# One core, a streaming encoder layer with 64 experts: two accumulators in HBM for even and odd blocks, empty places passed over, one gate product moved ahead

## What is computed

```python
def moe(x, w_router, router_bias, w_exp_gu, w_exp_down, w_sh_gu, w_sh_down):
    scores = jax.nn.sigmoid(jnp.einsum("td,de->te", xt, w_router))
    _, idx = lax.top_k(scores + router_bias, MOE_TOPK)          # 6 of 64 experts
    gate = jnp.take_along_axis(scores, idx, axis=-1)
    gate = gate / gate.sum(-1, keepdims=True) * ROUTED_SCALE
    routed = routed_experts(xt, idx, gate, w_exp_gu, w_exp_down)
    shared = swiglu(xt, w_sh_gu, w_sh_down)
    return (routed + shared).reshape(B, L, D)
# x <- LN2(ALPHA*x + MoE(x))
```

## Time and profile before

| | us |
|---|---|
| time before, median of 3 | 2080.77 (2078.91 to 2081.96) |
| the profiled execution: its own time | 2079.63 |
| its span | 2077.8 |
| PE busy | 1959.6 (94%) |
| DVE, ACT, POOL busy | 929.9, 562.7, 618.8 |
| expert loop, first product to last | 1269.5 to 2030.1 |
| from there to the span's end | 47.7 |

### The profile page before, as it was taken

One profiled execution on the slowest core, in us unless ns is written; L12 is line 12 of the kernel. 1 busy time (PEld: TensorE's weight loads), 2 busy tenths in 40 slices (PEclk: granted clock), 3 DMA queues, 4 the chain that ended last, 5 costly groups with the idle time before them and its releaser, 6 DMA issues.

```text
span 2077.8 us, 23451 instructions
## 1 busy us (share of the span) xinstructions
PE 1959.6 (94%) x7658; PEld 1084.7 (52%) x7658; DVE 929.9 (45%) x2467; ACT 562.7 (27%) x1147; POOL 618.8 (30%) x792
## 2 busy tenths in 40 slices
PE   8998999999999999999999899999999999999990
PEld 6786645666555665556555463444444444444440
DVE  4374465999765533030344743233332332332324
ACT  2223554562566640030233000111111111111114
POOL 0042000101220001101223254545445555555444
PEclk9999999999999999999999999999999999999995
DMA  6031212110110011134211406999999999999995
GB/s 189 3 38 14 64 41 102 41 47 5 26 26 3 1 31 48 44 132 126 103 61 48 155 31 217 376 369 373 381 373 375 378 373 376 375 373 377 375 364 193
DMA packets 130467, 365.09 MB, mean 176 GB/s; under 512 B 34641, under 2 KB 82514, under 8 KB 112594
## 3 DMA queue, kind: packets, MB, share of 16 engines
q1 hardware_dynamic: 105250, 289.80, 37.2%
q0 software_dynamic: 23328, 72.90, 13.6%
q10 hardware_dynamic: 1808, 1.33, 0.2%
HBM read 310.82 MB, written 53.04 MB: 175 GB/s over the span
## 4 chain that ended last, share of the span: by engine, by line
PE 55%; DMA 19%; DVE 8%; issue 7%; POOL 7%; ACT 2%; POOLq 0%; SPq 0%; DVEq 0%; ACTq 0%
DMA arena<-x_d,tid 17%; PE psum L630 11%; PE psum L774 9%; PE psum L792 6%; PE psum L645 4%; POOL arena L1293 3%; PE psum L845 3%; PE psum L444 3%; POOL acc_d L1287 2%; PE psum L479 2%; PE psum L708 2%; ACT arena L1341 2%; DVE arena L2264 2%; DMA acc_d<-arena,sid 2%; PE psum L491 2%
## 5 line engine op out<-in xcount | busy, mean ns | idle before, releaser
L1341 ACT ACTIVATE arena<-psum 128x512 f32<-128x512 f32 (+8 forms) x643 | 286.0, 486 | 1086.6 <-PE psum L918 429.7
L918 PE MATMUL psum<-arena 128*128 128x512 f32 x1088 | 484.3, 598 | 27.8 <-DVE arena L2264 24.9
L918 PEld LDWEIGHTS psum<-arena 128*128 128x128 f32 x1088 | 201.6, 190 | 267.2 <-issue 265.0
L1293 POOL DMA_INDIRECT arena<-x_d,tid x276 | 264.9, 960 | 85.8 <-issue 71.3
L932 PE MATMUL psum<-arena 128*128 128x512 f32 x544 | 244.7, 593 | 0.5 <-ACT arena L1341 0.5
L630 PE MATMUL psum<-arena 128*128 128x384 f32 (+1 forms) x768 | 239.7, 471 | 0.2 <-DMA arena<-in_w_glu 0.2
L2314 DVE TENSOR_TENSOR arena<-arena,psum 128x256 f32<-128x256 f32 x68 | 28.6, 421 | 457.7 <-ACT arena L1341 457.7
L630 PEld LDWEIGHTS psum<-arena 128*128 128x128 f32 x768 | 144.5, 190 | 94.7 <-issue 10.9
L774 PE MATMUL psum<-arena 128*128 128x384 f32 (+1 forms) x576 | 177.7, 472 | 1.1 <-DVE arena L2075 1.1
L2264 DVE STREAM_TRANSPOSE arena<-arena 128x256 f32<-128x256 f32 x272 | 150.3, 610 | 54.7 <-DMA arena<-x_d,tid 53.7
L932 PEld LDWEIGHTS psum<-arena 128*128 128x128 f32 x544 | 103.5, 190 | 130.0 <-issue 129.4
(11 more groups left out here) (313 smaller groups left out, 2148.1 us busy)
## 6 DMA issues: line engine op xcount, KB each, us to landing
arena<-in_w_exp_gu SPq DMA_DIRECT2D x69, 2048.0 KB, 10.4
arena<-in_w_exp_down SPq DMA_DIRECT2D x68, 1024.0 KB, 10.8
arena<-in_w_in SPq DMA_DIRECT2D x24, 512.0 KB, 4.5
arena<-in_x_prompt SPq DMA_DIRECT2D x10, 512.0 KB, 4.2
arena<-x_d,tid POOLq DMA_INDIRECT x276, 8.8
arena<-in_w_glu SPq DMA_DIRECT2D x16, 256.0 KB, 4.9
arena<-in_w_attn_proj SPq DMA_DIRECT2D x16, 256.0 KB, 4.5
arena<-in_w_out SPq DMA_DIRECT2D x1, 4096.0 KB, 14.4
```

What stands on the lines that cost most here:

```text
L918: last = mm(psum[:, 2, :], xgT[u][:, k, :], ewg[u][:, k, :], start=k == 0, stop=k == DK - 1)
L1293: pool.indirect_dma_start(xg[u][:, g, :], None, x1_d.rearrange("t (a f) -> (t a) f", a=4), bass.IndirectOffsetOnAxis(ap=tid[u][:, g:g + 1] ...
L1341: return act.activation(dst, src, fn, **kw)
```

## The change

There are now two accumulators, `acc_d[0]` for even blocks and `acc_d[1]` for odd ones. The first starts as before; the second is cleared whole from ACT's queue, in the GLU stage at about 304 us. POOL no longer waits for the scatter before. At the end, SP loads both for each tile (18 loads), and PE adds them: for each half of 512 columns, the identity times the one, then the identity times the other, in the same PSUM banks. Moments and scaling read the sum there, and the norm's weight is read from SBUF.

Gathers and scatters get a bounds check: a row number above the last token is passed over without an error. For an empty place then no row is fetched or added; the buffer keeps what an earlier block left there, its gate is zero, and the row is not stored.

`gate_shared(2)` moves on DVE ahead of the first five `slots`.

```diff
-        acc_d = dram("acc_d", (ACC, DM))
+        acc_d = [dram(f"acc{u}_d", (ACC, DM)) for u in range(2)]
...
+        odd_sums = at(15424, NT, DM)
+        total = lambda i: psum[0:rows(i), 2 + 2 * (i % 3):4 + 2 * (i % 3), :].rearrange("p b n -> p (b n)")
...
+            for i in range(NT):
+                r = rows(i)
+                pe.wait_ge(s(f"acc_loaded{i}"), 32)
+                if i >= 3:
+                    pe.wait_ge(s("scaled"), i - 2)
+                for j in range(2):
+                    for part_ in (x1, odd_sums):
+                        last = mm(psum[0:r, 2 + 2 * (i % 3) + j, :], ident[0:r, 0:r],
+                                  part_[0:r, i, j * 512:(j + 1) * 512], start=part_ is x1, stop=part_ is odd_sums)
+                last.then_inc(s("total_ready"), 1)
...
-                ld(x1[0:rows(i), i, :], acc_d[tok(i), :], f"acc_loaded{i}")
+                for u, part_ in enumerate((x1, odd_sums)):
+                    ld(part_[0:rows(i), i, :], acc_d[u][tok(i), :], f"acc_loaded{i}")
...
             def scatter(u, rows_):
-                pool.indirect_dma_start(acc_d, bass.IndirectOffsetOnAxis(ap=sid[u][:, 0:1], axis=0), rows_, None,
+                pool.indirect_dma_start(acc_d[u], bass.IndirectOffsetOnAxis(ap=sid[u][:, 0:1], axis=0), rows_, None,
+                                        bounds_check=T - 1, oob_is_err=False,
                                         compute_op=ALU.add).then_inc(s(f"y_stored{u}"), 16)
...
-                                            bass.IndirectOffsetOnAxis(ap=tid[u][:, g:g + 1], axis=0)
-                                            ).then_inc(s(f"xg_loaded{u}"), 16)
+                                            bass.IndirectOffsetOnAxis(ap=tid[u][:, g:g + 1], axis=0),
+                                            bounds_check=4 * T - 1, oob_is_err=False).then_inc(s(f"xg_loaded{u}"), 16)
...
                     pool.wait_ge(s("y_half"), n * 2 + 2)
-                    pool.wait_ge(s(f"y_stored{1 - u}"), ip * 16 + 16 + 16 * u)
                     carry_wait()
                     scatter(u, yb[u])
...
                         half = slice(j * 512, j * 512 + 512)
-                        act.dma_start(acc_d[T:ACC, half], zeros).then_inc(s("acc_cleared"), 16)
+                        act.dma_start(acc_d[1][:, half].rearrange("(b p) f -> p b f", p=DEC),
+                                      zeros[0:DEC].unsqueeze(1).broadcast_to([DEC, ACC // DEC, 512])
+                                      ).then_inc(s("acc_cleared"), 16)
+                        act.dma_start(acc_d[0][T:ACC, half], zeros).then_inc(s("acc_cleared"), 16)
...
             gate_shared(1)
             dve.wait_ge(s("x1_stored"), 16 * NT)
+            gate_shared(2)
             for i in range(NT + 1):
-                if 2 <= i + 1 < NT and i > 0:
+                if 3 <= i + 1 < NT:
                     gate_shared(i + 1)
...
-                r, x = rows(i), x1[0:rows(i), i, :]
-                dve.wait_ge(s(f"acc_loaded{i}"), 16)
+                r, x = rows(i), total(i)
+                dve.wait_ge(s("total_ready"), i + 1)
```

More of the change, by code:

```diff
@@ L234, in layer_program @@
         fin = at(47104, NT, 6)
-        weight = psum[:, 0:2, :].rearrange("p b n -> p (b n)")
+        odd_sums = at(15424, NT, DM)
+        total = lambda i: psum[0:rows(i), 2 + 2 * (i % 3):4 + 2 * (i % 3), :].rearrange("p b n -> p (b n)")
         eps = at(47160, 1)
@@ L1125, in _ @@
                 sp.wait_ge(s("base_ready"), i + 1)
-                ld(acc_d[tok(i), :], x1[0:rows(i), i, :], "base_stored")
+                ld(acc_d[0][tok(i), :], x1[0:rows(i), i, :], "base_stored")
             for q, name in enumerate(("ln2_g", "ln2_b")):
@@ L1261, in _ @@
                 tt(x, x, ln1[0:r, 1, :], ALU.add).then_inc(s("x1_ready"), 1)
-            pool.wait_ge(s("acc_cleared"), 16 * 4)
+            pool.wait_ge(s("acc_cleared"), 16 * 6)
             pool.wait_ge(s("dump_ready"), 2)
             for u in range(2):
-                if u == 1:
-                    pool.wait_ge(s("y_stored0"), 16)
-                pool.indirect_dma_start(acc_d, bass.IndirectOffsetOnAxis(ap=sid[u][:, 0:1], axis=0), ln1[:, u, :],
+                pool.indirect_dma_start(acc_d[u], bass.IndirectOffsetOnAxis(ap=sid[u][:, 0:1], axis=0), ln1[:, u, :],
                                         None, compute_op=ALU.add).then_inc(s(f"y_stored{u}"), 16)
@@ L1326, in _ @@
                 pool.wait_ge(s("y_half"), n * 2 + 2)
-                pool.wait_ge(s(f"y_stored{1 - u}"), last_pair * 16 + 16 + 16 * u)
                 carry_wait()
@@ L1640, in _ @@
             half_y(1, last_pair * 2 + 2)
-            act.wait_ge(s("ln2_loaded"), 32)
-            for j in range(2):
-                f(psum[:, j, :], ln2[:, 0, j * 512:(j + 1) * 512]).then_inc(s("weight_placed"), 1)
             moments = [0]
@@ L1656, in final_std @@
                 if i in MOMENTS_BY_SCALAR:
[L1657 to L1658 removed]
+                    x, unread = total(i), psum[0:r, 0:2, :].rearrange("p b n -> p (b n)")
+                    act.wait_ge(s("total_ready"), i + 1)
                     moment(f(unread, x, ACT.Copy, accum_out=m(4)))
@@ L2351, in scale_by_weight @@
             def scale_by_weight(i):
-                r, x = rows(i), x1[0:rows(i), i, :]
+                r, x, y, weight = rows(i), total(i), x1[0:rows(i), i, :], ln2[:, 0, :]
                 if i == 0:
-                    dve.wait_ge(s("weight_placed"), 2)
+                    dve.wait_ge(s("ln2_loaded"), 32)
                 if i in MOMENTS_BY_SCALAR:
                     dve.wait_ge(s("std_ready"), NT + i + 1)
-                    stt(x, x, fin[0:r, i, 5:6], weight[0:r, :], ALU.add, ALU.mult).then_inc(s("scaled"), 1)
+                    stt(y, x, fin[0:r, i, 5:6], weight[0:r, :], ALU.add, ALU.mult).then_inc(s("scaled"), 1)
                 else:
                     dve.wait_ge(s("var_ready"), NT + by_vector_no(i))
-                    stt(x, x, fin[0:r, i, 0:1], weight[0:r, :], ALU.subtract, ALU.mult).then_inc(s("scaled"), 1)
+                    stt(y, x, fin[0:r, i, 0:1], weight[0:r, :], ALU.subtract, ALU.mult).then_inc(s("scaled"), 1)
                     dve.wait_ge(s("std_ready"), NT + i + 1)
```

4 lines of the change are left out of this document (1 added, 3 removed).

## The result

| | before | after |
|---|---|---|
| median time, us | 2080.84 (2078.91 to 2081.96, 4 runs) | 2111.41 (2109.79 to 2114.61, 4 runs) |
| span of the profiled execution | 2077.8 | 2112.7 |
| first product of the loop | 1269.5 | 1283.05 |
| loop, first product to last | 760.6 | 771.6 |
| a block | 11.185 | 11.347 |

The ratio is 1.0148, 95% interval 1.0134 to 1.0163: slower by 1.5%, and outside the forecast range of 2048 to 2089. The 34.9 us of span fall into three parts that can be read off the table: 13.6 us lost before the loop, 11.0 us in it, 10.4 us behind it. Only the last was forecast. The profiled execution of after was the slowest of its four (2114.61 us), so the spans differ by 34.9 us where the medians differ by 30.6.

A forecast was written before the change was run, and what follows sets the result against it. The prediction took the expert loop to be bound by the DMA engines, with PE 0.67 us a block behind. Its terms, -10 - 1 + 8.5 = -2.5 us, gave a forecast of 2079 us, range 2048 to 2089.

The forecast's parts named there:

- The clearing: Before the loop, at about 304 us: writing 4.98 MB more from ACT's queue costs 0; 12 if idle DMA cover were gone.
- Passed-over places: Expert loop: 2176 of 8704 places (25%) no longer fetched or added; the loop gains 10.5 us, taken as 10.
- Uneven sharing: Expert loop, the forecast's own case: fixed partitions, a dropped entry not shared out anew; 2072 to 2086 us, chance 0.51.
- The term of -10: Expert loop: gain taken from passing over empty places, 10 us, with bounds of 0 and 45.6.
- The sign given for this case: Expert loop, uneven sharing: DMA share falls to about 0.95 of all engines while the period stays near 11.03 us.
- the slow rival: Expert loop: passed places cost as much engine time as full ones, as dummy packets; 2091 us, chance 0.14.
- The even rival: Expert loop: engines share the empty places evenly, 33 us gained, time 2055; chance 0.30.
- The scatter chain: Expert loop: POOL's wait for the scatter before goes, gathers issue some 2.5 us sooner; worth nothing alone.
- POOL's instructions: Expert loop: bounds checks may lengthen five indirect DMAs a block; up to 0.7 us more on each is hidden, cost 0.
- The gate product: Before the loop: PE's 9.5 us idle at 1162 goes, but waiting for POOL's token lists leaves a 1 us gain.
- The end: After the loop: loads start 5.9 us sooner, but adding two accumulators on PE costs +8.5 us; bounds +5.7 to +12.
- slow restart: At the end: PE, idle for 9 us with its clock at half, loses 1.3 us on the first sum.

The follow-up runs named there:

- e1: The kernel after, with the second accumulator's clearing issued from SyncE's queue instead of ACT's: 2096.55 us, ratio 1.0076.
- e2: e1 without the two bounds checks, every empty place fetched and added as before: 2090.08 us, ratio 1.0045.
- e6: The kernel before with only the third shared gate product moved ahead of the first five slots on DVE: 2081.39 us, ratio 0.9996.
- e5: e1 with a block's places spread over the partitions, empty ones falling evenly on sets of four partitions and four 32 above: 2058.55 us, ratio 0.9897.
- e10: e1 with places spread instead over runs of eight neighbouring partitions, as a counter-test to e5: 2101.88 us, ratio 1.0103.
- e11: e2 with each scatter adding only places 0 to 95 of its block, so part of the result is left out: 2056.83 us, ratio 0.9872.
- e9: e1 with the bounds check of the scatters alone, places in order: 2102.64 us, ratio 1.0106.
- e13: e6 (one accumulator and its waits) with the bounds check of the scatters alone, places in order: 2084.74 us, ratio 1.0025.
- e8: e1 with the bounds check of the gathers alone, places in order: 2090.21 us, ratio 1.0046.
- e7: e4 with places spread as in e5, one accumulator and the old end: 2044.84 us, ratio 0.9836.
- e3: e1 with the waits between scatters put back, both checks and both accumulators kept: 2094.96 us, ratio 1.0065.
- e4: e6 with both bounds checks, places in order, one accumulator, its waits and the old end: 2079.31 us, ratio 0.9995.
- e12: e13 with the places spread as in e5, one accumulator, scatter check alone: 2057.10 us, ratio 0.9877.

## Why the prediction was wrong

The loss of 1.48% splits by ratios into four: the clearing on ACT's queue 0.72% (after against e1, 15 us), the checks with places in order 0.31% (e1 against e2, 6.5 us, their gain at the end included), two accumulators 0.49% (e2 against e6, 10 us; 13 us more at the end, and the loop no longer), the gate product -0.04%. Each ratio is known to about 0.15%, so a difference of two is uncertain by about 0.2%: the first is clear, and of the second little more than its sign.

**The clearing** failed as a step, and was the largest miss. I costed it at 0 because the page's slices show the DMA engines nearly idle there, and gave 12 us as its price if that cover were gone. The engines' room was real: PE waited for no transfer in that stage, in after or in e1. What I left out was the engine that issues: behind the first 2432 KB each issue on ACT's queue held ACT for 2.06 to 7.67 us, with the DMA engines full, and PE waited 10.80 us for ACT. My own list of costs names the queue ("written from ACT's queue") and then prices only the bytes. The row that bore on it was in the trace: the issues of before grow from 0.34 to 1.28 us within four. It was not among the rows that I had picked. That the price of 12 is near the measured 13.6 to 15 is luck: its mechanism was another.

**Passed-over places.** Uneven sharing, the case that I took, was the true one: e5 against e10 (728.0 and 773.7) fit fixed sets, and e11 (730.8 against 773.3 in e9) shows that a shorter list is shared anew. The weights did lie on all engines, with 16 of their packets under way at once for 12% of 1300 to 1990 us in before. And they landed no sooner with the empty places in order (gate-up, 10.4 us after the issue in before and e9, 10.5 in after, 10.6 in e13). That it is the engine of the first places that keeps its rows, and that it would gain 0.30 us a block on its gathers, stays an estimate: no view shows a single engine. The term of -10 failed all the same, in sign: +8 to +11 measured. The failed step is the premise that an engine that gets no relief stays as it was. It did not: weight packets and scattered rows got longer, one MB of weights cost 2.51 us of engine time rather than 2.38, and e13 has 310 long weight packets where e2 has 5. The sign given for this case, a DMA share of about 0.95, came out at 0.99. I had also counted on 20 blocks with 96 tokens or fewer, where a gather loses one of its four groups; the gather check alone gave 1.7 us (e8), and 5 on top of the scatter check (e1 against e9). My bounds had 0 on the losing side, though no row excluded a loss. "A dropped entry still goes through as a dummy packet" was right as to the packet, in the slow rival, but its price was wrong: those of a scattered row took 9 to 24 ns, not 328.

**The even rival** (33 us from the loop) described a kernel that was one table of numbers away: e7's loop gives 27.0, e5's 32.6. With e7's 10.79 us a block, 0.27 us over PE's 10.52 are left. PE's waits are down to 5.9 us in 700, but q0 and q1 together still take 100.7% of the engines' time there, so what bounds the rest is not shown.

**The scatter chain** at nothing: right. POOL's wait for scatters went, and e2's loop is that of before; e3 and e13 show no effect clear of the spread of profiles either.

**POOL's instructions** at 0: right. A checked gather took 1016 ns rather than 960, a scatter 1632 rather than 1634, far inside the 0.7 us that were hidden.

**The gate product** at -1: 0.7 read from e6's timeline, by the mechanism given: PE comes early to the placing matmuls and goes on at the pace of POOL's lists. Only its first wait there ends with DVE's one-hot matrices and not with a list.

**The end** at +8.5, measured +10.4, within its bounds. Step by step: loads 5.7 us sooner (5.9 forecast); 4.8 us to the first pair (4.8); the first sum after 6.6 us rather than 3.44 + 1.3; then 27.54 to the ninth (27.5), and 14.7 to the end (14.8). The term that was mis-sized is the slow restart. Windows of after:

```profile
2064.00:2072.00 8.00, 8.00 (x13) 3.43 (x14) 1.46 (x3) 0.00 (x0) 0.00 (x0) 0.65 1.03 417
2072.00:2098.00 26.00, 26.00 (x61) 10.63 (x59) 14.78 (x27) 15.73 (x29) 11.73 (x5) 1.00 0.69 256
```

The granted clock was 0.65 over the first eight microseconds, and the first tile took 6.59 us instead of 3.44: about 3 us, not the 1.3 of a restart after a gap of about the same length in the earlier trace rows. Without the checks the end is 60.4: the early landing of the empty block was worth 2.3 us here, and 5.0 with one accumulator (e4 against before).

**What stays open:** why weight packets take up to 4.4 times as long when the engines are uneven. The runs tie it to the order of the empty places (e12 against e13) and rule out the number of accumulators (e13 against e9). The run that was to make uneven engines without tiny packets (e11) did not, so that both are needed together is not excluded; and what the packets contend for, no view here shows.

## What to carry to other kernels

Price a transfer three times: its bytes on the DMA engines, its issue on the engine whose queue it is put in, and who waits for that engine; the first cost nothing that could be measured here, and the second and third together about 15 us. Passed-over scatter rows shortened this loop only with the empty places spread over the sets (744.1 in e12, against 772.3 in order in e13 and 761.2 without the check in e6), so lay out the data so that the empty ones fall on all the sets; in this kernel that order of places is the difference between +12 and -16 us for the scatters alone. And an accumulator that is split to remove a wait needs its merge priced at the end, where nothing hides it: 15.5 us here, for a wait whose removal brought nothing clear of the noise in a loop that the DMA engines bound.

## What the runs showed of the hardware

- An issue on ACT's queue took from 0.34 us up to 7.67 us, and ACT ran no activation from 305.6 to 321.9 us (after). The long one moves 256 KB and stands behind the second of two issues of 2432 KB. On SyncE's queue, the issues behind the same two took 7.83 to 9.84 us (e1).
- A passed-over row of a scatter still makes a packet, of 8 bytes and 9 to 24 ns (e9, after), and the queue has as many packets a block as before (332 in after against 333). In place order such a list of 128 makes the loop longer (773.3 in e9 against 760.0), while a list of 96 rows makes it shorter (730.8, e11).
- A packet of 4 KB took 328 ns when it was added to HBM and 159 ns when it was gathered (medians, before).
- With the empty places in order and passed over by the scatters, 4% (e13) of the 16 KB weight packets took over 1.3 times their 611 ns, up to 2.7 us, in clusters; with nothing passed over under 0.1% (e2), with the empty places spread 1.6% (e12). Fewer than 16 packets were under way for 10.8%, 0.1% and 3.8% of the time in these three.
- After 9.3 us without work at the end, TensorE's clock stood at 0.65 of full speed over its first 8 us; after 10.8 us in the GLU stage at 0.58 over 8 (both in after).
